# Decoder step on one core: two neighbouring pages of the paged cache share two tiles, on even and on odd partitions

## The reference

```
past_k = pool_k[page_table].reshape(b, PAST_LEN, B_HEADS, 2, HEAD_DIM)
past_v = pool_v[page_table].reshape(b, PAST_LEN, B_HEADS, B_VDIM)
s = einsum('bqhce,bkhce->bchqk', q, k) * (e ** -0.5)
a = softmax(where(mask, s, -inf), axis=-1)
attn = a[:, :, 0] - lam * a[:, :, 1]
out  = einsum('bhqk,bkhe->bqhe', attn, v)
```

## Time and profile before

| | us |
|---|---|
| median of 3 runs | 1640.33 (1638.16 to 1640.35) |
| the profiled execution | 1636.09 |
| its span | 1634.2 |
| stage of attention in it, about | 698 to 1117 |
| PE busy over the whole span | 1490.0 (91%) |
| DMA records: all, of which of the queue that SP issues | 217143, 217026 |

### The profile page before, as it was taken

How to read it: one execution, slowest core, us unless ns; L and a number is a source line. 1 busy time by engine, 2 the same in 40 slices (tenths; PEclk the granted TensorE clock), 3 DMA queues, 4 the chain that set the end, 5 groups by cost and what they waited for, 6 DMA issues and landing times.

```text
span 1634.2 us, 32198 instructions
## 1 busy us (share of the span) xinstructions
PE 1490.0 (91%) x12323; PEld 1296.1 (79%) x12323; DVE 833.5 (51%) x1617; ACT 567.9 (35%) x1020; POOL 203.2 (12%) x246
## 2 busy tenths in 40 slices
PE   4899999999998999978988878877979999999996
PEld 3688999999996777745656555555969999999995
DVE  0322323332345444345655456564689973699664
ACT  2422222221124121144445344543254441354323
POOL 0200000000001100010000000000036620455100
PEclk8899999999998999989999999997989999999998
DMA  9994222233322233378999898974222322333221
GB/s 335 387 314 162 78 84 83 77 92 89 90 67 72 78 93 106 107 210 263 287 281 277 267 268 244 275 234 129 78 59 82 95 74 83 106 94 97 68 77 58
DMA packets 217143, 245.98 MB, mean 151 GB/s; under 512 B 10239, under 2 KB 154105, under 8 KB 217026
## 3 DMA queue, kind: packets, MB, share of 16 engines
q1 hardware_dynamic: 217026, 244.43, 48.9%
HBM read 237.31 MB, written 7.08 MB: 150 GB/s over the span
## 4 chain that ended last, share of the span: by engine, by line
PE 71%; SPq 9%; DMA 7%; DVE 6%; issue 5%; ACT 2%; POOL 0%; ACTq 0%; DVEq 0%
PE ps L307 28%; PE ps L960 20%; PE ps L1496 10%; SPq L1716 4%; SPq L1693 4%; DMA kv<-in_cache_diff_k_dram 4%; PE ps L1802 3%; DMA wada<-in_w_ada_dram 2%; PE ps L291 2%; PE ps L1272 2%; DVE ring_lo L952 1%; PE ps L1876 1%; PE ps L1814 1%; PE ps L1858 1%; PE ps L1841 1%
## 5 line engine op out<-in xcount | busy, mean ns | idle before, releaser
L276 ACT ACTIVATE whi<-w 128x1024 fp32r<-128x1024 f32 (+1 forms) x92 | 102.6, 1116 | 426.7 <-PE ps L307 350.4
L282 DVE TENSOR_TENSOR wlo<-w,whi 128x1024 fp32r<-128x1024 f32 (+1 forms) x92 | 120.2, 1308 | 253.1 <-ACT whi L276 252.8
L952 DVE TENSOR_TENSOR ring_lo<-ring_raw,ring_hi 128x512 fp32r<-128x512 f32 x177 | 164.8, 963 | 25.9 <-ACT ring_hi L938 21.8
L1802 PEld LDWEIGHTS ps<-ident,kv 128*128 128x128 f32 (+1 forms) x896 | 98.9, 146 | 87.1 <-issue 62.7
L307 PE MATMUL ps<-hhi,whi 128*128 128x288 f32 x768 | 166.0, 298 | 0.9 <-ACT tmp L773 0.9
L307 PE MATMUL ps<-hhi,wlo 128*128 128x288 f32 x768 | 164.4, 296 | 0.0
L307 PE MATMUL ps<-hlo,whi 128*128 128x288 f32 x768 | 164.3, 296 | 0.0
L1802 PE MATMUL ps<-ident,kv 128*128 128x128 f32 (+1 forms) x896 | 122.3, 278 | 44.3 <-DMA kv<-in_cache_diff_k_dram 30.8
L938 ACT ACTIVATE ring_hi<-ring_raw 128x512 fp32r<-128x512 f32 (+1 forms) x199 | 112.9, 611 | 98.9 <-DMA ring_raw<-in_ffn_w_out_dram 88.0
L2026 DVE COPY KC<-ps 128x512 f32<-128x512 f32 (+2 forms) x128 | 75.2, 588 | 109.7 <-PE ps L1802 88.0
L307 PEld LDWEIGHTS ps<-hhi,whi 128*128 128x128 f32 x768 | 123.4, 189 | 6.1 <-issue 4.8
(11 more groups left out here) (256 smaller groups left out, 3185.7 us busy)
## 6 DMA issues: line engine op xcount, KB each, us to landing
wada<-in_w_ada_dram SPq DMA_DIRECT2D x18, 2048.0 KB, 13.0
kv<-in_cache_diff_k_dram SPq DMA_DIRECT2D x128, 256.0 KB, 4.4
kv<-in_cache_diff_v_dram SPq DMA_DIRECT2D x128, 256.0 KB, 3.5
w<-in_ffn_w_in_dram SPq DMA_DIRECT2D x44, 512.0 KB, 4.0
ring_raw<-in_ffn_w_in_dram SPq DMA_DIRECT2D x88, 256.0 KB, 3.0
w<-in_w_qkv_dram SPq DMA_DIRECT2D x24, 512.0 KB, 3.9
kv<-in_cache_win_k_dram SPq DMA_DIRECT2D x32, 384.0 KB, 5.4
kv<-in_cache_win_v_dram SPq DMA_DIRECT2D x32, 384.0 KB, 7.4
```

The costliest lines, as they stand in the source:

```text
L276: nc.scalar.activation(whi[:, slot, 0:w], w32[:, slot, 0:w], ACT.Copy).then_inc(ph.hi, 1)
L282: nc.vector.tensor_tensor(wlo[:, slot, 0:w], w32[:, slot, 0:w], whi[:, slot, 0:w].bitcast(F32), ALU.subtract).then_inc(ph.lo, 1)
L952: eng.tensor_tensor(lo_of(g, i)[:, 0:n, :], ring_raw[g % 2][i][:, 0:n, :], ring_hi[g % 2][i][:, 0:n, :].bitcast(F32), ALU.subtract).then_i ...
L1802: mm = pe.transpose(ps[:, f % 2, k * kw:(k + 1) * kw], kv(c % 2)[0:kw, k, f * P:(f + 1) * P], ident[0:kw, 0:kw])
```

## The change

Each page is now written to 64 partitions instead of 128. Page k of a quarter goes to the partitions of its own parity (k even: partitions 0, 2, ... 126; k odd: 1, 3, ... 127), and there to the two tiles of its pair: two neighbouring positions, 2t and 2t + 1 of the page, lie behind one another in one partition. So a piece that is moved in one go is 4 KB and there are 64 of them, where it was 2 KB and 128. Keys and values are placed in the same way. The number of transfers, their bytes, their waits and all the other engines' instructions are the same.

```
@@ -1712,8 +1712,8 @@
                     for k in range(n):
-                        src = pool[is_v][ds(page[k], 1), :, :].rearrange("a p c -> (a p) c")
-                        eng.dma_start(slot[:, k, :], src).then_inc(s, 16)
+                        src = pool[is_v][ds(page[k], 1), :, :].rearrange("a (p t) c -> (a p) t c", t=2)
+                        eng.dma_start(slot[k % 2:P:2, k // 2 * 2:k // 2 * 2 + 2, :], src).then_inc(s, 16)
```

## The result

The changed kernel takes 1659.8 us (median of 4 runs, 1654.7 to 1661.7) against 1640.1 before: 1.0112 times, 95% interval 1.0086 to 1.0138. It is slower, as forecast, but by 19.7 us and not by 45: the forecast time of 1685 was too high by 25, and the step that gave it was wrong. That the direction came out right is luck, since it came by another cause.

The account below looks back on a forecast made before the run. It took the attention stage as held in turn by SP, transfers and PE; 72 us more DMA work made 441, over 0.95 is 464 us, 45 more than 419; 1636.1 + 45 = 1681, plus 4.2 gives 1685, range 1635 to 1730.

Parts of the forecast that it names:

- What bounds the stage: Attention stage, 419 us: held in turn by SP, the transfers and PE; SP last from 841 to 869 us.
- DMA price after: Page transfers on the DMA engines: 1.06 us per page, from mixer A's 96-partition far keys, 0.28 us more than now.
- The first rival: Page transfers: even and odd partitions as good as all 128, larger pieces help, 0.69 us a page; 1632 us, chance 0.17.
- a burst's slow first pieces: Page transfers now: 0.10 us between 0.78 us per page in a burst and 0.68 at full flow.
- SP's cost: Issue of a page transfer on SP: ends 0.31 and 0.43 us, taken as 0.33, with the same registers as now.
- The third: Rival: partitions cost nothing, SP's issue rises to 0.43 us, 18 us more where SP is last; 1654 us, chance 0.06.
- The second rival: Page transfers: xstok's price and the 0.10 us, 1.22 us per page; 1728 us, the range's upper end, chance 0.18.
- The sum: Attention stage: 441 us of DMA work at a share of 0.95 gives 464 us, 45 more than 419.
- The clock of PE: PE in the attention stage: granted at 0.96, longer waits may lower it somewhat; nothing added for it.
- What would show it: Attention stage profile: digits 9 at 225 to 250 GB/s, key-page wait over 60 us, 16384 fewer packets.
- The last sign: Attention stage: if not longer than 419 us, the 96-partition price does not hold for evenly spread partitions.

Follow-up runs that it names:

- The shapes kernel: One kernel in which each sequence loads its pages in another of six shapes, as before and as changed among them; 1664.1 us, read only for its rows.
- the far loads: Kernel before with mixer A's far loads in five shapes (64, 96 or 128 partitions, source stepped or in one piece); 1637.0 us, read only for its rows.
- with SP lightened: Page numbers read for the keys held and reused for the values, in the kernel before (1619.7 us) and in the changed kernel (1631.9 us).
- the kernel with the switch off: Kernel before with nc.dge_precook off for the page transfers alone, 128 partitions kept; 1659.2 us, ratio 1.0111.
- the halves: Changed kernel with each page in 64 neighbouring partitions (0 to 63 or 64 to 127) instead of every second one; 1690.1 us, ratio 1.0303.

## Why the prediction was wrong, point by point

- What bounds the stage. SP, the transfers and PE in turn, and SP last from 841 to 869 us: right as far as the runs show (35 us more of SP work cost 22, and 22 us less of DMA work bring 13.8), and it is through SP that the change acts.
- DMA price after, "I take the row nearest in kind, 1.06 us": this step failed. It measured 0.81 to 0.83, the work of the DMA engines in the stage 356 us and not 441, and the transfers did not become last. I ranked the rows by the count of partitions ("as soon as a transfer has fewer than 128 partitions"), and took 96 neighbouring ones for the kin of 64 spread ones. The shapes kernel and the far loads show that the set counts: every second partition flows like all 128 (397 and 387 GB/s), halves (232) and the lower 96 (233 to 262) do not. The first rival had this, with 0.17; I kept the ranking by the count. The 0.10 us that I put down to a burst's slow first pieces is shown in part: from 859.5 to 860.0 us the kernel before moved 90 GB/s at a share of 0.61, 1.78 us for each 256 KB, but from 863.5 to 864.0, at the start of the next load, 106 GB/s at 0.30, 0.74 us.
- SP's cost, "The ends are therefore 0.31 and 0.43 us. I take 0.33": failed too, in value and in its end. It is 0.475. The reason given (the same registers) had no row behind it, and a row of the kernel before showed a transfer to 64 partitions that is dearer (0.59 against 0.40 us): the one to 64 partitions at the start of the program beside its neighbour to 128 (timeline of SP, start us, us):

```profile
4.17 0.40 SPq L1318 DMA_DIRECT2D xtok<-in_x_prompt_dram  x1
4.62 0.59 SPq L1319 DMA_DIRECT2D xstok<-in_x_sample_dram  x1
```

  I used `xstok` for its rate and did not look at its issue.
- The rivals. The third (the partitions cost nothing, SP's issue rises) is what happened, given 0.06 and 1654 us. With 0.142 in place of 0.1 us its own sum is 22 x 8 x 0.142 = 25 us; measured 19.7, and 12.2 with SP lightened. That a longer issue is enough is shown by the kernel with the switch off: 0.475 us for each page transfer, and 1659.2 us. The first rival's half, that the sets are equal for the engines, was right as well, but its 0.09 us a page from larger pieces did not come: none in the stretches with only pages, 10 us of 366 in the stage. The second rival, with 0.18, gave a page `xstok`'s price and the 0.10 us, 1.22 in all; its (369 + 256 x 0.44) / 0.95 = 507 us of stage and 1728 us are the upper end of the range. No run shows that price for every second partition: they measured 0.81 to 0.83 us, and even halves 1.14.
- The sum. Work divided by a share of 0.95 was a sound way where the transfers are last: the halves reached exactly that share. For the changed kernel it did not apply, since the work did not grow. The clock of PE was left out of the sum, with the remark that it may fall; it was granted at 0.93 for 0.96 in the stage, and at 0.91 in the halves' stage of 472 us. Whether longer waits lower it, no run separates.
- What would show it. What the third and the first rival said of single rows came: an issue well above 0.33 us (0.43 said, 0.475 measured), and every second partition as good as all 128 (397 GB/s beside 387). The signs of the forecast itself did not: digits of 8 at 247 to 267 GB/s and not 9 at 225 to 250, a wait for key pages of 37.8 us and not over 60. The last sign, a stage not longer than 419 us, could not find the error, since the stage grew by SP. The packets fell by 16384, as said.

The range of 1635 to 1730 held 1659.8, and the chances were on the right side, but the forecast size was more than twice the measured one.

## What to carry to other kernels

Price a changed transfer on two accounts: what the issuing engine pays per transfer, and what the DMA engines pay per byte; where one queue issues everything, as here, 0.14 us per transfer outweighs what the other gains. Look for the row that shares the property, not the count: for the rate here that was how the partitions are spread (397 GB/s for every second one, 232 for 64 neighbours), for the issue it was `xstok`, the other transfer to 64 partitions (0.59 us, 0.40 for its neighbour to 128). And where a transfer touches 96 neighbouring partitions, try all 128, even if the rest is thrown away: here it made the kernel 13.8 us faster.

## What the runs showed of the hardware that was not expected

- In this kernel's programs a page transfer to 64 or 32 partitions takes SP 0.47 us where one to 128 takes 0.33; with `nc.dge_precook` off, transfers to 128 partitions cost the same 0.142 us more (0.475). Two pieces per partition cost 0.13 more (0.60 to 0.61). Why 64 and 32 partitions are dearer to issue, and mixer A's 96 (380 and 427 ns in the median) less so, stays open.
- Right behind a load of pages that SP issues at 0.475 us each, 32 of mixer A's transfers take 0.58 us to issue (0.59 in the kernel with the switch off), where they take 0.43 behind pages issued at 0.333.
- 128 partitions with 4 KB pieces at a step of 32 KB in the source flow at 401 to 414 GB/s, as from a source in one piece (410).
- Pages to every second partition in 4 KB pieces cost the DMA engines what pages to all 128 in 2 KB pieces do: 0.83 against 0.82 us over some 15 us of pages alone.
- 96 neighbouring partitions flow at 233 to 262 GB/s, 128 with a third more bytes at 401 to 414.
- 35 to 41 us of work on SP in this stage, put in three ways, cost 19 to 22 us of the kernel's time.
